# Scatters cut in column halves, a third rows buffer, and another order at the first and last expert tile

## The reference

```python
def hierarchical_moe(h, w_group, b_group, w_er, b_er, w_gate, w_up, w_down):
    t = h.reshape(B * S, D)
    ...
    expert_id = g_sel[:, None] * EXPERTS_PER_GROUP + top_i
    comb = jnp.sum(jax.nn.one_hot(expert_id, N_EXPERTS) * top_p[..., None], axis=1)
    hg = jnp.einsum('td,edf->tef', t, w_gate)
    hu = jnp.einsum('td,edf->tef', t, w_up)
    act = jax.nn.silu(hg) * hu * comb[..., None]
    out = jnp.einsum('tef,efd->td', act, w_down)
...
    h = h + hierarchical_moe(n2, ...)
```

## Time and profile before

| | |
|---|---|
| Median of 3 runs | 1541.28 us (1540.48 to 1542.13) |
| The profiled execution | 1542.55 us |
| Its span | 1540.6 us |
| PE busy | 1454.0 us (94%) |
| DVE busy | 1088.8 us (71%) |
| ACT busy | 768.2 us (50%) |
| POOL busy | 500.4 us (32%) |
| Share of `DMA out<-e_y,dest` in the chain that ended last | 14% |
| Scatters on POOL (L2280), 31 | 72.9 us, mean 2353 ns |
| ACT on 128 x 512 (L1205), mean | 615 ns |
| Expert tiles | from about 1204 us to the end |

### The profile page before, as it was taken

One profiled execution on the slowest core, in us unless ns is written; L12 is line 12 of the kernel. 1 busy time (PEld: TensorE's weight loads), 2 busy tenths in 40 slices (PEclk: granted clock), 3 DMA queues, 4 the chain that ended last, 5 costly groups with the idle time before them and its releaser, 6 DMA issues.

```text
span 1540.6 us, 19925 instructions
## 1 busy us (share of the span) xinstructions
PE 1454.0 (94%) x7190; PEld 1203.5 (78%) x7190; DVE 1088.8 (71%) x1516; ACT 768.2 (50%) x1269; POOL 500.4 (32%) x387
## 2 busy tenths in 40 slices
PE   5999999999999998899999999999997699998995
PEld 5987888987889887677677788888885588887874
DVE  4328999999999956775749833336353799898883
ACT  5247323336421535776443443223245488887873
POOL 2310222463424366000135533333231245242322
PEclk9998999999999998999999999999998699999997
DMA  5210111113211043210175344444426896988973
GB/s 192 63 34 1 41 47 37 42 42 109 83 42 42 28 143 131 65 46 29 41 234 175 91 143 143 144 144 148 164 84 241 318 280 176 326 246 289 279 243 66
DMA packets 89473, 199.91 MB, mean 130 GB/s; under 512 B 11168, under 2 KB 32928, under 8 KB 87072
## 3 DMA queue, kind: packets, MB, share of 16 engines
q1 hardware_dynamic: 76560, 158.01, 30.5%
q0 software_dynamic: 8928, 32.51, 8.8%
q10 hardware_dynamic: 3888, 8.13, 1.4%
HBM read 206.22 MB, written 39.58 MB: 160 GB/s over the span
## 4 chain that ended last, share of the span: by engine, by line
PE 68%; DMA 16%; DVE 7%; ACT 4%; issue 3%; POOL 1%; ACTq 0%; SPq 0%; DVEq 0%; POOLq 0%
PE ps L775 19%; PE ps L776 19%; PE ps L777 19%; DMA out<-e_y,dest 14%; PE ps L1004 4%; PE ps L994 2%; DVE dist L1705 1%; DMA w_raw<-in_w_in 1%; PE ps L942 1%; DMA xin<-in_x 1%; PE ps L955 1%; DVE f_sum L1816 1%; DMA e_x<-n_dram,token 1%; PE ps L957 1%; DVE sig L1816 1%
## 5 line engine op out<-in xcount | busy, mean ns | idle before, releaser
L2140 POOL TENSOR_TENSOR w_lo<-w_raw,w_hi 128x512 fp32r<-128x512 f32 (+1 forms) x184 | 254.9, 1391 | 599.6 <-ACT w_hi L1205 523.0
L1205 ACT CAST w_hi<-w_raw 128x512 fp32r<-128x512 f32 (+1 forms) x184 | 111.9, 615 | 403.2 <-PE ps L777 352.7
L775 PE MATMUL ps<-w_hi,n_hi 128*128 128x512 f32 (+2 forms) x704 | 244.2, 347 | 1.9 <-ACT ro L1364 1.6
L776 PE MATMUL ps<-w_lo,n_hi 128*128 128x512 f32 (+2 forms) x704 | 241.9, 344 | 0.0
L777 PE MATMUL ps<-w_hi,n_lo 128*128 128x512 f32 (+2 forms) x704 | 241.8, 344 | 0.0
L2083 DVE TENSOR_TENSOR e_lo<-e_raw,e_hi 128x2048 fp32r<-128x2048 f32 x93 | 212.6, 2291 | 27.1 <-ACT e_hi L1594 27.0
L1594 ACT CAST e_hi<-e_raw 128x2048 fp32r<-128x2048 f32 x93 | 177.4, 1915 | 29.9 <-PE ps L777 17.3
L1744 DVE MAX8 small<-dist 128x8 f32<-128x384 f32 (+5 forms) x192 | 171.8, 895 | 6.6
L775 PE MATMUL ps<-n_hi,w_hi 128*128 128x512 f32 x416 | 164.2, 395 | 4.6 <-POOL w_lo L2140 2.5
L1745 DVE MATCH_REPLACE8 dist<-small,dist 128x384 f32<-128x384 f32 (+5 forms) x192 | 168.1, 876 | 0.0
L776 PE MATMUL ps<-n_lo,w_hi 128*128 128x512 f32 x416 | 162.2, 390 | 0.0
(11 more groups left out here) (275 smaller groups left out, 2864.4 us busy)
## 6 DMA issues: line engine op xcount, KB each, us to landing
e_raw<-in_w_gate SPq DMA_DIRECT2D x64, 512.0 KB
e_raw<-in_w_up SPq DMA_DIRECT2D x64, 512.0 KB
e_raw<-in_w_down SPq DMA_DIRECT2D x32, 1024.0 KB
w_raw<-in_w_in SPq DMA_DIRECT2D x120, 256.0 KB, 2.7
a_raw<-att_dram SPq DMA_DIRECT2D x16, 512.0 KB, 3.4
a_raw<-ret_dram SPq DMA_DIRECT2D x16, 512.0 KB, 3.3
w_raw<-in_w_out SPq DMA_DIRECT2D x24, 256.0 KB, 3.2
w_raw<-in_w_in SPq DMA_DIRECT2D x40, 128.0 KB, 2.3
```

The costliest lines, as they stand in the source:

```text
L775: mm(out, a[0], b[0], start=first, stop=False, skip_group_check=skip)
L776: mm(out, a[0], b[1], start=False, stop=False, skip_group_check=skip)
L1205: nc.scalar.copy(w_hi[c % NH][:, :width], split_from(c)[:, :width]).then_inc(hi_ready, 1)
L2140: G.tensor_tensor(w_lo[c % NH][:, :width], split_from(c)[:, :width], w_hi[c % NH][:, :width].bitcast(F32), ALU.subtract).then_inc(lo_ready, 1)
```

## The change

1. **Scatters.** `dest` becomes two arrays (twice the row, plus 0 or 1) and `out` is also seen as rows of 512. `add_rows` issues two indirect DMAs of 128 rows of 2 KB, the left and the right half of the columns; each waits for its own half of the tile before. `e_y` has a third buffer, and `rows_out` waits for both halves of three tiles before.
2. **First tile.** `token` is made before `fresh` and `owner`. SP waits for the gather of the second tile before it loads that tile's weights. PE runs turn_rows(0) ahead of slot_weights; in the first step it turns the second tile's rows in the middle of gate_up. DVE's slot_weights comes after the splits of tile 0, and in the first step ACT and DVE split part 0 of tile 1's weights before its rows.
3. **Last tile.** Its down weights are split before its Silu, into the buffer that held part 0 of the tile before (`split_at`). Its down product signals after each bank, ACT evicts it in halves, and each half is scattered as it is ready.

```diff
-        dest = sb("dest", [P, 32], U32)
+        dest = [sb(f"dest{j}", [P, 32], U32) for j in range(2)]
+        out_halves = out.rearrange("r (j n) -> (r j) n", j=2)
...
-        e_y = [sb(f"e_y{i}", [P, D], at=nt_at + 8 * W3 + 8 * D + i * 4 * D) for i in range(2)]
+        e_y = [sb(f"e_y{i}", [P, D], at=nt_at + 8 * W3 + 8 * D + i * 4 * D if i < 2 else wr_at + 16 * W3 + 24 * D + 16 * FF) for i in range(3)]
...
+        def split_at(e, i, j):
+            return e[i.parity][j] if j < 2 or not (i + 1).reached(NTILE) else e[(i + 1).parity][0]
...
+                if i.n == 1:
+                    sp.wait_ge(ex_in[1], 16)
...
-            def gate_up(i):
+            def gate_up(i, ks=range(KT)):
...
-                for k in range(KT):
+                for k in ks:
...
-                last.then_inc(gu_full, 1)
+                if ks[-1] == KT - 1:
+                    last.then_inc(gu_full, 1)
...
+                    if n == 0 and (i + 1).reached(NTILE):
+                        last.then_inc(ey_full, 1)
                 last.then_inc(ey_full, 1)
+            turn_rows(Step(0))
             slot_weights()
-            turn_rows(Step(0))
 
             def work(i):
                 if i.reached(1):
                     turn_act(i - 1)
-                if not (i + 1).reached(NTILE):
+                if not i.reached(1):
+                    gate_up(i, range(0, 4))
                     turn_rows(i + 1)
-                if not i.reached(NTILE):
+                    gate_up(i, range(4, KT))
+                elif not (i + 1).reached(NTILE):
+                    turn_rows(i + 1)
+                    gate_up(i)
+                elif not i.reached(NTILE):
                     gate_up(i)
...
+            def last_rows_out(i):
+                n = tile_at(i)
+                for j in range(2):
+                    act.wait_ge(ey_out[i.buffer][j], 16 * i.third)
+                    act.wait_ge(ey_full, i.n + 1 + j)
+                    A(e_y[i.buffer][:, j * BANK:(j + 1) * BANK], ps[:, B_Y + j * BANK:B_Y + (j + 1) * BANK], ACT.Identity,
+                      scale=p_slot[:, n:n + 1]).then_inc(ey_read, 1)
+
             def rows_out(i):
                 act.wait_ge(ey_full, i.n + 1)
-                if i.reached(2):
-                    act.wait_ge(ey_out[i.parity], 16 * i.half)
+                if i.reached(3):
+                    for j in range(2):
+                        act.wait_ge(ey_out[i.buffer][j], 16 * i.third)
...
-                if not (i + 1).reached(NTILE):
+                if not i.reached(1):
+                    w_part(i + 1, 0)
+                    x_part(i + 1)
+                elif not (i + 1).reached(NTILE):
                     x_part(i + 1)
                     w_part(i + 1, 0)
+                else:
+                    w_part(i, 2)
...
+            bk.wait_full(dve, ("token",))
+            V.tensor_scalar(token[:], bank(("token",), 32), -1.0, 0.0, ALU.add, ALU.max).then_inc(token_done, 1)
             seq(V.tensor_scalar(fresh[:, 0:1], small[:, 384:385], 1.0, None, ALU.min))
             V.tensor_scalar(owner[:], small[:, 384:416], float(NE - 1), None, ALU.min).then_inc(owner_done, 1)
-            bk.wait_full(dve, ("token",))
-            V.tensor_scalar(token[:], bank(("token",), 32), -1.0, 0.0, ALU.add, ALU.max).then_inc(token_done, 1)
...
-            V.scalar_tensor_tensor(dest[:], small[:, 464:496], -1.0, small[:, 384:416], ALU.add, ALU.add).then_inc(dest_done, 1)
+            seq(V.scalar_tensor_tensor(small[:, 464:496], small[:, 464:496], -1.0, small[:, 384:416], ALU.add, ALU.add))
+            for j in range(2):
+                inst = V.tensor_scalar(dest[j][:], small[:, 464:496], 2.0, float(j), ALU.mult, ALU.add)
+            inst.then_inc(dest_done, 1)
...
             w_part(Step(0), 0)
-            slot_weights()
             x_part(Step(0))
             w_part(Step(0), 1)
+            slot_weights()
...
-                pool.wait_ge(ey_read, i.n + 1)
-                if i.reached(1):
-                    pool.wait_ge(ey_out[(i - 1).parity], 16 * ((i - 1).half + 1))
                 n = tile_at(i)
-                G.indirect_dma_start(out=out, out_offset=bass.IndirectOffsetOnAxis(ap=dest[:, n:n + 1], axis=0),
-                                     in_=e_y[i.parity][:], in_offset=None, compute_op=ALU.add).then_inc(ey_out[i.parity], 16)
+                for j in range(2):
+                    pool.wait_ge(ey_read, i.n + 1 + (j if (i + 1).reached(NTILE) else 0))
+                    if i.reached(1):
+                        pool.wait_ge(ey_out[(i - 1).buffer][j], 16 * ((i - 1).third + 1))
+                    G.indirect_dma_start(out=out_halves, out_offset=bass.IndirectOffsetOnAxis(ap=dest[j][:, n:n + 1], axis=0),
+                                         in_=e_y[i.buffer][:, j * BANK:(j + 1) * BANK], in_offset=None,
+                                         compute_op=ALU.add).then_inc(ey_out[i.buffer][j], 16)
```

More of the change, by code:

```diff
@@ L404, in program @@
         slot_done = sem("slot_done")
-        ey_full, ey_read, ey_out = sem("ey_full"), sem("ey_read"), [sem(f"ey_out{i}") for i in range(2)]
+        ey_full, ey_read, ey_out = sem("ey_full"), sem("ey_read"), [[sem(f"ey_out{i}{j}") for j in range(2)] for i in range(3)]
         dest_done, p_done2 = sem("dest_done"), sem("p_done2")
@@ L762, in _ @@
             each_step(load_expert, NTILE - 1)
-            for i in range(2):
-                sp.wait_ge(ey_out[i], 16 * ((NTILE + 1 - i) // 2))
+            for i in range(3):
+                for j in range(2):
+                    sp.wait_ge(ey_out[i][j], 16 * ((NTILE + 2 - i) // 3))
         @block.tensor
@@ L1171, in down @@
                         last = three(ps[:, B_Y + n * BANK:B_Y + (n + 1) * BANK], (at_hi[:, k, :], at_lo[:, k, :]),
-                                     (e_hi[b][2][:, ws], e_lo[b][2][:, ws]), k == 0, k == 1)
+                                     (split_at(e_hi, i, 2)[:, ws], split_at(e_lo, i, 2)[:, ws]), k == 0, k == 1)
+                    if n == 0 and (i + 1).reached(NTILE):
+                        last.then_inc(ey_full, 1)
                 last.then_inc(ey_full, 1)
+            turn_rows(Step(0))
             slot_weights()
-            turn_rows(Step(0))
             def work(i):
@@ L1591, in w_part @@
                     act.wait_ge(gu_full, i.n - 1)
-                if j == 2 and i.reached(1):
+                if j == 2 and (i + 1).reached(NTILE):
+                    act.wait_ge(gu_full, i.n)
+                elif j == 2 and i.reached(1):
                     act.wait_ge(ey_full, i.n)
-                nc.scalar.copy(e_hi[i.parity][j][:], e_raw[i.buffer][j][:]).then_inc(ehi_done[j], 1)
+                nc.scalar.copy(split_at(e_hi, i, j)[:], e_raw[i.buffer][j][:]).then_inc(ehi_done[j], 1)
             def x_part(i):
@@ L1633, in work @@
                     w_part(i + 1, 1)
-                w_part(i, 2)
+                    w_part(i, 2)
             each_step(work, NTILE - 1)
@@ L1637, in _ @@
             a_part(Step(NTILE - 1))
-            rows_out(Step(NTILE - 1))
+            last_rows_out(Step(NTILE - 1))
         @block.vector
@@ L2082, in w_part @@
                 dve.wait_ge(ehi_done[j], i.n + 1)
-                V.tensor_tensor(e_lo[i.parity][j][:], e_raw[i.buffer][j][:], e_hi[i.parity][j][:].bitcast(F32), ALU.subtract).then_inc(elo_done[j], 1)
+                V.tensor_tensor(split_at(e_lo, i, j)[:], e_raw[i.buffer][j][:], split_at(e_hi, i, j)[:].bitcast(F32), ALU.subtract).then_inc(elo_done[j], 1)
             def x_part(i):
@@ L2303, in _ @@
             add_rows(Step(NTILE - 1))
-            for i in range(2):
-                pool.wait_ge(ey_out[i], 16 * ((NTILE + 1 - i) // 2))
+            for i in range(3):
+                for j in range(2):
+                    pool.wait_ge(ey_out[i][j], 16 * ((NTILE + 2 - i) // 3))
             for j in range(3):
```

3 lines of the change are left out of this document (1 added, 2 removed).

## The result

The changed kernel takes 1531.03 us as a median of 7 runs (1529.24 to 1535.97), the kernel before, run beside it, 1540.75 (1538.78 to 1545.83). The ratio is 0.9938, with a 95% interval of 0.9923 to 0.9953: faster, by 9.7 us. The forecast was 1524.0, 17.3 us faster, in a range of 1518 to 1535. A later set gave 1530.71 against 1540.76, ratio 0.994 (0.9927 to 0.9954).

The account below looks back on a forecast made before the run. PE was taken as the bound, busy 94% of the span, with 13.1 us of holes in steady flow. Gains of 12.0 + 2.0 + 3.3 = 17.3 us took 1541.28 to 1524.0 us, own range 1519 to 1528, full range 1518 to 1535.

Parts of the forecast that it names:

- Holes gone by two half chains and a third buffer: Steady flow of expert tiles: PE's holes, 13.1 us, mostly vanish; 12.0 us taken, bounds 4 and 13.1.
- 9.3 of the 13.1 go even if the chain is no faster: Steady flow: the third rows buffer alone forgives one more tile of lag, removing 9.3 us of holes.
- the first rival: Halves no faster than wholes beside loads: buffer 9.3, tail 0.5, head 2, so 1529.5 us; chance 0.22, shared with another rival.
- The chain's step: Scatters in steady flow: each half chain steps 9.5 to 10.5 us beside loads, 6 in quiet, mean under PE's 9.34.
- Added DMA time: Scatters in half rows cost the DMA engines 0.3 us more per tile, bounds 0 and 3.3, fitting in free time.
- the slower rival: Accumulating scatters cost by the row, not the byte: 3.3 us more per tile, 1590 us in all; chance 0.11.
- Head: First expert tile: the reordered start gains 2.0 us; bounds 4 gained, 2 lost.
- e_hi for tile 1 comes at about 1215.9: First tile: ACT's split of tile 1's weights starts at about 1215.9 instead of 1217.74.
- The loads have 11 us until that Silu is due: First tile: tile 1's weight loads, issued 3.9 us later, have 11 us until tile 0's Silu.
- what would prove it wrong: Signs against the forecast, among them the Silu of tile 0 waiting behind tile 1's weights.
- Last tile: End of the kernel: early weight split and half scatters gain 3.3 us; bounds 0.5 and 3.9.
- the rivals without faster halves or without head and tail: Two rivals, 1529.5 us if halves are no faster, 1529.3 if head and end give nothing; 1527 to 1536, chance 0.22.

Follow-up runs that it names:

- x4: The kernel before with scatters in column halves and nothing else, so two rows buffers; 1532.28 us, ratio 0.995.
- x3: The kernel before with a third rows buffer and nothing else, scatters whole; 1540.16 us, ratio 0.9993.
- x7: The changed kernel, SP wait kept, but in the first step ACT and DVE handle tile 1's weights after the Silu of tile 0; 1529.82 us, ratio 0.9932.
- x1: The changed kernel without SP's wait for the second tile's gather; 1525.61 us, ratio 0.990.
- x2: The changed kernel with every order of the head as before and no SP wait; 1525.58 us, ratio 0.990.
- x8: x2 plus gate_up(0) in two parts with turn_rows(1) between, and weights before rows on ACT and DVE in the first step; 1525.67 us, ratio 0.9906.
- x10: x8, but POOL issues the gathers of tiles 2 and 3 only after turn_rows(0); 1525.04 us, ratio 0.9901.
- x11: The changed kernel run again unchanged, on the chip of x10; 1530.71 us.

## Why the prediction was right, and where it was not

**Holes gone by two half chains and a third buffer, 12.0 us of 13.1.** Right in size: 12.7 in the trace. That the halves carry most of it was right as well (x4: 8.7 of the 13.1 without the third buffer). Its bound below was not: "9.3 of the 13.1 go even if the chain is no faster" fell with x3, where 6.7 went and 6.3 came back at the end. The step took a lag as forgiven that is only put off, because it looked at who waits for a buffer and not at what the last scatter waits for. With it the first rival was mis-sized: with x3's 0.9 us in place of the 9.3 its sum is 0.9 + 0.5 + 2.0, and by that estimate halves no faster than wholes would have given not 1529.5 but about 1538. That the 12.0 came out so near is in part luck, since this bound and the mean step below were both wrong.

**The chain's step.** Expected were 4.4 to 5 us from issue to landing of a half in quiet, a step of 9.5 to 10.5 beside loads, and a mean step under 9.34. In quiet it was 4.7 us for the last ones and 5.7 before them (the chain above). Of all the changed kernel's halves the profile says (minimum, median, maximum):

```profile
DMA to landing us min/median/max: 4.7/8.1/10.7
```

But it finds the landing of only 11 of the 62; for the 31 whole ones it has 6.0, 8.0 and 12.1. In x7, whose steady flow has no hole either, it finds 20 halves and the slowest took 12.5. So no shorter landing beside loads is shown. POOL's issues say more. Where a scatter ended POOL's wait before 1494, the step from one issue to the next of the same half was 10.3 us on the mean (25 steps, the slowest 12.6), that of the whole ones 10.25 (24 steps, 12.85). So, as far as the releasers in brackets can be trusted, the rival's premise holds, that a half waits as long as a whole beside loads, and its conclusion does not. Counting every step, the left halves went from 1243.42 (tile 0) to 1493.37 (tile 26), 9.61 each, the right ones from 1246.24 to 1489.46 (tile 25), 9.73, the whole ones from 1237.48 to 1491.85 (tile 25), 10.17. Half chains fall behind PE's 9.35 as well, but by 0.3 us per tile instead of 0.8, and here the buffers covered that; in x1's trace and with two buffers in x4 they did not. The mean under 9.34 was wrong. Why the mean step is shorter is not shown; that two halves are under way together is the likely reason. The Trainium skill's rule against a cut in two ("DMA: Bandwidth & Descriptors", "Rules for kernel authors") is about two transfers to disjoint partition halves, which by it share the same engines and serialize. The traces agree in this much, that a half was no quicker beside loads and the two cost the engines 0.49 us more than the whole. What was bound here was a chain of landings, of which the rule does not speak.

**Added DMA time, 0.3 us per tile taken, bounds 0 and 3.3.** Measured 0.49; the share in 1224 to 1494 went from 0.87 to 0.92, under the 0.95 that was named. The window's row, engines and then clock, DMA share and GB/s:

```profile
1224.00:1494.00 270.00, 265.49 (x1300) 224.34 (x1301) 248.45 (x172) 230.87 (x200) 165.60 (x78) 0.99 0.92 279
```

So the slower rival, a cost by the row, did not come about at 2 KB. POOL's busy time was put at 167 us for this window and is 165.6.

**Head, 2.0 us gained (bounds 4 gained, 2 lost).** This step failed, by 7 us and past its own bound: it costs about 5 (x1 and x2 against the changed kernel, 5.4). PE's part was right: gate_up(0) starts 14.6 us after the token matmuls, 14.9 was forecast and 17.5 it had been (its first matmul stands at 1216.39 in the trace of before, not at the prediction's 1216.74), and ends 1.7 us earlier. The term that failed is "e_hi for tile 1 comes at about 1215.9": 17.0 us after the token matmuls, measured 22.0. Of the 5 us, 0.7 are the later landing of the gather; the rest is the length of the load. It was put at 5.9 us from issue to first use, for which the prediction gives no row; it took the loads behind it at the stage's mean of 2.7 us per MB. In five traces the first split of tile 1's weights came 10.2 (after), 10.7 (x1), 10.9 (x8), 9.9 (x10) and 9.7 us (x11) after SP's first load was issued, and no later than 11.6 in the kernel before, whatever else was moving. The trace before did not contradict such a length: issued at 1206.13, these weights were used at 1217.74 without a wait, which bounds the load at 11.6 us and shows nothing shorter. "The loads have 11 us until that Silu is due" was counted, but it is w_part that stands in front of the Silu, and x_part(1), e_lo and x_lo with it, 5 us of work after the load. Then the 4.67 us hole cost more than itself: PE's granted clock was 0.50 in 1228 to 1232 against 1.00 in 1220 to 1224, before the hole, and that tile took 11.46 us instead of 9.85 (the window, read as the row above):

```profile
1228.00:1232.00 4.00, 3.49 (x13) 3.20 (x14) 4.00 (x4) 3.22 (x4) 0.81 (x1) 0.50 1.03 413
```

The prediction had named this wait among what would prove it wrong.

**Last tile, 3.3 us (bounds 0.5 and 3.9).** 3.1 measured. PE went on 2.09 us after turn_act(30), as forecast 2.1, at the high clock; a half landed in 4.74 to 4.75 us, L was taken as 4.7; and the last scatter waits for the second half of tile 29 as worked out. What holds that half was taken wrong: not POOL's issues but the landing of tile 28's second half at 1513.94. It goes out 4.4 us after turn_act(30), where 4.0 was forecast, so the error is small. The high clock was in part luck: gaps of this length were followed by the low one in other traces (last section).

**The median.** 12.7 + 3.1 - 5 = 10.8 against 9.7 measured by the medians. The 1531.03 us lie in the stated range of 1518 to 1535, but not in the forecast's own 1519 to 1528: they fall into the band of the rivals without faster halves or without head and tail, 1527 to 1536, though neither is what happened. The halves and the tail gave what was forecast, and the head took 5 us back. Since the unprofiled executions of the kernel before differ by 7 us (1538.78 to 1545.83) and its profiled one lay 1.8 above their median, its mean hole is probably smaller than 13.1; no second trace of it was taken, so that stays open.

## What to carry to other kernels

A buffer more between a producer and a chain of dependent transfers does not shorten the chain: ask what the last transfer waits for, because a lag that nobody waits for in the middle is paid at the end. Where each transfer must wait for the one before, cutting it into independent parts can pay as long as the issuing engine has time (here two parts gained 8.8 us; four, with POOL full, lost 66). Before a load is held back for the sake of another transfer, take its length from its own place in the trace, not from the stage's mean rate, and look for what stands behind its first use in an in-order list.

## What the runs showed of the hardware that was not expected

- The first expert loads ran at 3.5 us of engine share per MB (x10: 0.92 MB in 0.80 x 4 us) with gathers in 17.4% beside them, the whole stage's at 2.7. The cause is open.
- Cutting accumulating scatters from 4 KB to 2 KB and 1 KB rows cost the DMA engines 0.49 and 0.59 us per tile for 128 and 256 rows more; POOL's issue takes 1.55 us at least for a whole, a half or a quarter alike.
- A PE gap of 4.67 us was followed by about 4.5 us at the low clock. Gaps of 1.7 to 1.9 us went both ways: the granted clock was 1.00 behind those of 1349.46 and 1408.64 in the kernel before and of 1512.38 in the changed one, but 0.63 in 1420 to 1424 of the kernel before, 0.66 in 1461 to 1465 of x3 and 0.59 in 1234 to 1238 of x10. In these three the next tile took 11.0 to 11.1 us instead of 9.35. What tells the two kinds apart is not shown.
